# Retention values: the mean over a head's channels taken off the weights by GpSimd, in the recurrent passes, in place of a centring matmul on TensorE

## The reference, cut to what matters

```python
def group_norm_heads(z, eps):
    mu = jnp.mean(z, axis=-1, keepdims=True)
    var = jnp.mean(jnp.square(z - mu), axis=-1, keepdims=True)
    return (z - mu) * lax.rsqrt(var + eps)

# retention_mixer, 8 heads: q, k with 64 channels, v with 128; chunks of 128 tokens
    def step(R, inp):
        qc, kc, vc = inp
        s = jnp.einsum('bihd,bjhd->bhij', qc, kc) * decay_mask
        inner = jnp.einsum('bhij,bjhe->bihe', s, vc)
        cross = jnp.einsum('bihd,bhde->bihe', qc * q_decay, R)
        R = R * chunk_decay + jnp.einsum('bjhd,bjhe->bhde', kc * k_decay, vc)
        return R, inner + cross
    o = group_norm_heads(o, RET_GN_EPS).reshape(B, T, RET_V_WIDTH)
    return jax.nn.silu(g) * o
```

## Time and profile before

| | us |
|---|---|
| median of three runs (2323.48 to 2326.77) | 2326.6 |
| the profiled execution's own time | 2324.7 |
| its span, first to last instruction | 2322.9 |
| TensorE busy | 2285.8 (98%) |
| TensorE weight loads | 1883.9 (81%) |
| VectorE busy | 1399.6 (60%) |
| GpSimd busy | 916.8 (39%) |
| ScalarE busy | 752.9 (32%) |

### The profile page before, as it was taken

The page is one execution under the profiler, slowest core; times in us unless marked ns, Lnnn a source line. Parts: engine busy times, 40 slices in busy tenths (PEclk is TensorE's granted clock), DMA queues, the critical chain, the costliest instruction groups (busy, mean ns, idle before and its releaser), DMA issues.

```text
span 2322.9 us, 33491 instructions
## 1 busy us (share of the span) xinstructions
PE 2285.8 (98%) x12764; PEld 1883.9 (81%) x12764; DVE 1399.6 (60%) x1632; ACT 752.9 (32%) x1243; POOL 916.8 (39%) x538
## 2 busy tenths in 40 slices
PE   7999999999999999999999999999999999999998
PEld 6788888888888888888888877888888887777776
DVE  7755374537543754576638895555551488756775
ACT  4311131122111211334325224444432445114442
POOL 3311231123112313403366457777744445422164
PEclk9999999999999999999999999999999999999999
DMA  3211211121111113663544422222156433211023
GB/s 148 80 55 46 74 55 55 55 74 55 55 55 65 64 46 117 204 225 136 190 148 136 175 94 82 82 82 82 64 196 213 144 123 100 67 57 43 31 82 118
DMA packets 71317, 230.65 MB, mean 99 GB/s; under 512 B 6800, under 2 KB 11024, under 8 KB 70672
## 3 DMA queue, kind: packets, MB, share of 16 engines
q1 hardware_dynamic: 40560, 138.76, 18.2%
q10 hardware_dynamic: 30624, 89.97, 10.5%
HBM read 182.04 MB, written 46.66 MB: 98 GB/s over the span
## 4 chain that ended last, share of the span: by engine, by line
PE 86%; DVE 7%; ACT 2%; issue 1%; DVEq 1%; POOL 1%; DMA 1%; POOLq 1%; ACTq 0%; SPq 0%
PE psg L771 7%; PE psg L776 7%; PE psg L778 6%; PE psg L639 4%; PE psg L644 4%; PE psg L643 4%; PE psa L1243 2%; PE psa L1245 2%; PE psa L1246 2%; PE psb L1243 2%; PE psb L1245 2%; PE psb L1246 2%; PE psa L871 2%; PE psb L858 1%; PE psg L733 1%; PE psg L1454 1%
## 5 line engine op out<-in xcount | busy, mean ns | idle before, releaser
L527 POOL CAST whi<-wraw 128x1024 fp32r<-128x1024 f32 (+1 forms) x144 | 166.7, 1158 | 1102.5 <-PE psg L771 512.2
L529 POOL TENSOR_TENSOR wlo<-wraw,whi 128x1024 fp32r<-128x1024 f32 (+1 forms) x144 | 370.6, 2574 | 20.8 <-issue 0.2
L771 PE MATMUL psg<-xhi,whi 128*128 128x512 f32 x640 | 259.2, 405 | 0.0
L778 PE MATMUL psg<-xhi,wlo 128*128 128x512 f32 x640 | 258.0, 403 | 0.0
L776 PE MATMUL psg<-xlo,whi 128*128 128x512 f32 x640 | 256.4, 401 | 0.0
L639 PE MATMUL psg<-xhi,whi 128*128 128x512 f32 x496 | 196.8, 397 | 4.0 <-DVE fg L2015 2.4
L644 PE MATMUL psg<-xhi,wlo 128*128 128x512 f32 x496 | 195.2, 394 | 0.0
L643 PE MATMUL psg<-xlo,whi 128*128 128x512 f32 x496 | 194.3, 392 | 0.0
L603 POOL TENSOR_TENSOR wlo<-wraw,whi 128x1024 fp32r<-128x1024 f32 (+1 forms) x50 | 111.9, 2239 | 140.0 <-ACT whi L2799 74.2
L771 PEld LDWEIGHTS psg<-xhi,whi 128*128 128x128 f32 x640 | 120.9, 189 | 26.1 <-issue 6.3
L778 PEld LDWEIGHTS psg<-xhi,wlo 128*128 128x128 f32 x640 | 120.8, 189 | 21.0 <-issue 1.0
(11 more groups left out here) (710 smaller groups left out, 5893.5 us busy)
## 6 DMA issues: line engine op xcount, KB each, us to landing
wraw<-w SPq DMA_DIRECT2D x208, 512.0 KB, 3.5
later_scratch<-stage ACTq DMA_DIRECT2D x40, 512.0 KB, 2.6
sraw<-w SPq DMA_DIRECT2D x16, 512.0 KB, 4.0
ff_scratch<-ring ACTq DMA_DIRECT2D x10, 512.0 KB, 2.6
ff_scratch<-ff ACTq DMA_DIRECT2D x10, 512.0 KB, 2.6
ff<-ff_scratch ACTq DMA_DIRECT2D x5, 1024.0 KB, 7.0
RV<-later_scratch SPq DMA_DIRECT2D x4, 1024.0 KB, 11.5
RG<-later_scratch SPq DMA_DIRECT2D x4, 1024.0 KB, 5.5
```

The costliest lines, as they stand in the source:

```text
L527: pool.tensor_copy(whi[:, u, 0:width], wraw[:, u, 0:width])
L529: pool.tensor_tensor(wlo[:, u, 0:width], wraw[:, u, 0:width], whi[:, u, 0:width].bitcast(F32), ALU.subtract).then_inc(w_ready, 1)
L771: mm = pe.matmul(ps[:, cols], whi[:, slot, w_cols], xhi[:, k, cols], start=(k == 0), stop=False)
L778: mm = pe.matmul(ps[:, cols], wlo[:, slot, w_cols], xhi[:, k, cols], start=False, stop=(k == KT - 1))
```

## The change

The two value blocks of each recurrent pass are split by a new function, `centre_block`. It adds up the 128 columns of each of the block's eight tiles by halving (three additions over 8 x 32 elements per partition, then five over 8 x 16, 8, 4, 2 and 1), scales the eight sums by 1/128, subtracts them from the weights (1024 elements), and then casts and subtracts as `split_block` does, with a drain between any two. The retention values then come out with no mean, and `ret_values` turns them with a plain transpose. The matrix `RC`, its DMA and its row in the constants are gone; the small buffer of the sums lies where it lay. GpSimd's loop over the passes has all 14 blocks of a pass in its body, where it had two.

```diff
+            def centre_block(i, u):
+                raw = wraw[:, u, :].rearrange("p (k c) -> p k c", c=P)
+                pool.wait_ge(w_landed[u], 16 * i + 16)
+                pool.wait_ge(w_used, 2 * i + u + 1)
+                pool.sem_inc(go, 1)
+                part = w_part
+                n = P // 4
+                pool.tensor_tensor(part[:, :, :], raw[:, :, 0:n], raw[:, :, n:2 * n], ALU.add)
+                for c in (2, 3):
+                    pool.drain()
+                    pool.tensor_tensor(part[:, :, :], part[:, :, :], raw[:, :, c * n:c * n + n], ALU.add)
+                n //= 2
+                while n:
+                    pool.drain()
+                    pool.tensor_tensor(part[:, :, 0:n], part[:, :, 0:n], part[:, :, n:2 * n], ALU.add)
+                    n //= 2
+                pool.drain()
+                pool.tensor_scalar(part[:, :, 0:1], part[:, :, 0:1], 1.0 / P, None, ALU.mult)
+                pool.drain()
+                pool.tensor_tensor(raw, raw, part[:, :, 0:1].broadcast_to([P, KT, P]), ALU.subtract)
+                pool.drain()
+                pool.tensor_copy(whi[:, u, :], wraw[:, u, :])
+                pool.drain()
+                pool.tensor_tensor(wlo[:, u, :], wraw[:, u, :], whi[:, u, :].bitcast(F32), ALU.subtract
+                                   ).then_inc(w_ready, 1)
...
-            split_blocks(2, B_BRW)
+            with pool.Fori(0, PAIRS) as p:
+                for q in range(RW_B // 2):
+                    for u in range(2):
+                        if q == VALUE_PAIR:
+                            centre_block(RW_B // 2 * p + q + 1, u)
+                        else:
+                            split_block(RW_B // 2 * p + q + 1, u)
...
-            sp.dma_start(RC[:, :], mats[:, M_CENT_RET, :]).then_inc(sem("rv_in"), 16)
...
-                    pe.wait_ge(sem("rv_in"), 16 * p + 32)
+                    pe.wait_ge(sem("rv_in"), 16 * p + 16)
...
-                    mm = pe.matmul(dst[:, c, :], RV[:, h, c * P:c * P + P], RC[:, :], start=True, stop=True)
+                    mm = pe.transpose(dst[:, c, :], RV[:, h, c * P:c * P + P], m(M_ID))
```

More of the change, by code:

```diff
@@ L56 @@
 NMAT = M_LVL + LEVELS
-M_CENT_RET = NMAT
 LATER = 10
@@ L63 @@
 RW_B, RW_T = 4 + LATER, 6 + LATER
+VALUE_PAIR = 3
 B_BRW, T_BRW = B_RW + RW_B * PAIRS, T_RW + RW_T * PAIRS
@@ L282, in build @@
         RKT, RS = tiles("RKT", 24, [P, NB, P]), tiles("RS", 25, [P, NB, P])
-        RP, RC = [tiles("RP0", 26, [P, NB, P]), spare("RP1", 6, [P, NB, P])], at("RC", arena + 27 * 4096 + 3072, [P, P])
+        RP = [tiles("RP0", 26, [P, NB, P]), spare("RP1", 6, [P, NB, P])]
+        w_part = at("w_part", arena + 27 * 4096 + 3072, [P, KT, P // 4])
         rraw = [tiles("rraw_first", 4, [P, 2, T]), tiles("rraw1", 18, [P, 2, T]), spare("rraw0", 0, [P, 2, T])]
@@ L3186, in constants @@
     t, s = i[:, None], i[None, :]
-    mats = np.zeros((NMAT + 1, P, P), np.float32)
+    mats = np.zeros((NMAT, P, P), np.float32)
     mats[M_ID] = np.eye(P)
@@ L3190, in constants @@
     mats[M_CENT] = np.eye(P) - same / CH
-    mats[M_CENT_RET] = np.eye(P) - 1 / P
     mats[M_BLK] = same
```

## The result

The change makes the kernel slower by 0.36%: the ratio of the times is 1.0036, with a 95% interval of 1.0027 to 1.0045. The median of 8 runs is 2333.34 us (2331.62 to 2336.9) against 2325.48 us (2323.48 to 2327.99, 8 runs too) of the kernel before. The interval makes the loss 6.3 to 10.5 us, 8.4 in the middle. The forecast was 2339.1 us, 12.5 more than the 2326.6 of the three runs that it started from; the sign and the range held, the size was too large. The profiled execution took 2333.42 us with a span of 2331.6, which is 8.7 over the span before.

The account below looks back on a forecast made before the run. TensorE, with 86% of the chain, was taken to bound the kernel. Waits of 9.6 us plus 4.2 of clock less 1.3 of retention made 12.5 us over the 2326.6 median: 2339.1 us, range 2327 to 2356.

Parts of the forecast that it names:

- The mechanism and the place: In each recurrent pass, GpSimd and VectorE exclude each other on SBUF; TensorE waits for `centre_block` at the third later feature.
- Block 7: Second value block of each pass: ends by 348 us, hidden with 4 us to spare before its feature at about 352.
- The scores: TensorE's scores in each pass, which wait for VectorE's preparation (L1729): claimed not to be late.
- The wait's size: TensorE's wait for the first value block: 2.4 us per pass, 9.6 us in four; bounds 1.6 and 3.3 per pass.
- The block's own length: A centred value block alone on GpSimd: 11.4 us, against 3.6 before.
- The turns: Block 6 beside VectorE's preparation: 0.45 us late start, then six long VectorE instructions slip in, 0.8 us added each, 4.8 in all.
- The clock: TensorE drops to the 1.2 GHz level behind new waits, 1.7 us each, counted in 2.5 passes: 4.2 us (bounds 0 and 6.8).
- Retention: Three junctions of retention passes, values turned by transposes: 0.43 us gained each, 1.3 us in all; bounds 0.8 and 5.9.
- The two heads of the first pass: Retention stage: their shorter turning saves nothing, since TensorE then waits 2.85 us for GpSimd until 962.35 and would wait longer.
- (a): Rival: GpSimd's short instructions needn't wait for VectorE's long ones, so no pass waits; 2325.3 us, or up to 2320.7; chance 0.13.
- (b): Rival: GpSimd's short instructions over eight rows cost 0.3 us more each, 2352.5 us, or 0.6 more, 2363.3; chance 0.15.
- (c): Rival within the forecast's range: waits never cost the clock, or are short; 2331.7 to 2334.9 us; chance 0.72 together with the forecast.

Follow-up runs that it names:

- `centre_only`: The changed kernel with the value blocks centred but the values still turned by the matmul with `RC`; ratio to the kernel before 1.0038 (1.0024 to 1.0052), 8.8 us.

## Why the prediction was right, and where it was off

**The mechanism and the place: right.** One wait per pass for the last subtraction of `centre_block`, at the first matmul of the third later feature. TensorE was ready 338.10 - 2.02 - 321.75 = 14.33 us after GpSimd's start (14.26 forecast). Block 7 was hidden: it ended at 350.09, 6.2 us before GpSimd could begin block 8 (4 forecast). The scores weren't late.

**The wait's size: 2.0 instead of 2.4.** The block's own length came out right, 11.32 against 11.4, but by two errors: the short instructions together took 0.3 us more than forecast (the scaling of 8 elements 0.24 for 0.23, the additions of 128 to 8 elements 1.93 for 1.58), and the subtraction of the means took 1.92 us where the row of another two-input subtraction over 1024 elements gave 2.39. The turns cost 4.90 instead of 5.25: six slips of 0.8 were forecast, in the rows it is 1.62 for two and 2.86 for the other four. Between two of VectorE's long instructions there stands a short copy (L1748), which I had left out; that GpSimd gains the missing 0.35 there is argued, not shown. And 0.13 us pass from GpSimd's end to TensorE's start. 16.22 + 0.13 - 14.33 = 2.02; four make 8.1, not 9.6.

**The clock: +1.7 net instead of 4.2.** This is the step that was mis-sized. 2.5 passes of four were counted; two had it in this profile, one in its second execution, one in `centre_only`: 4 of 12 waits of 2.0 us. And the count left out that the half level behind L1012, which stood in the kernel before, could go. With the rows as they were nothing told that it would. What a stretch costs, 1.7 us, was right. (Of the 5.8 us between forecast and median another 1.1 is the start: 2326.6 was the median of three runs, 2325.48 that of eight.) Here the rows spoke against the Trainium skill, and the runs still do: "TensorE: Matmul & The Clock Gate", section "HAM oscillation — how this bites in real kernels", lets only idle gaps longer than these cost the clock, and half-level stretches stood behind waits of 2.0 us. My 4.2 was no better a guide: 8 of the 12 waits of 2.0 us cost nothing.

**Retention: -1.35 us, forecast -1.3.** Junction by junction, -0.45 for -0.43. The two heads of the first pass gave nothing, but for another reason than the one given: TensorE waits for the values' copy by ScalarE (L1058 for `RVT`) 2.2 us where it waited 1.3, so the 0.9 us were turned into a wait before L1012 was reached.

**The rivals.** (a), that short instructions slip past VectorE's long ones for nothing, fell: beside VectorE's long ones they waited their turns. (b), that short instructions over eight rows are dear, fell too: 0.74 us for 256 elements as forecast; the row of the undisturbed block has nothing added. The Trainium skill, "GPSIMD Engine Reference", section "Performance pitfalls for Q7 kernels", prices small read commands; the estimate from its figure was some 0.7 us more for each instruction, which the 0.74 us row doesn't show. (c), waits without the clock's loss, 2331.7 to 2334.9 us, is the one that the time came to, 2333.3, and that is partly luck: the clock did cost 3.4 us behind two waits of the profiled run, and a stretch that went elsewhere, shorter waits and a lower start made up for it. I held (c) apart from the forecast only by name, and should have given the likeliest time nearer to it.

**Two slips in the sums.** Six times 0.97 us is 5.8, not 5.9, and with a fixed part of 0.30 us the wait comes to 3.0 to 3.2 us, not 3.3. The forecast hangs on neither.

## What to carry to other kernels

Work given to GpSimd is costed by its neighbours, not by its length: ask whether VectorE reads two SBUF tensors at that time, and add, for each of its long instructions, its hold less the gap that passes anyway (0.7 to 0.8 us here), however short the GpSimd instruction is that waits. The same ten added instructions a block cost 8 us in one slot of the pass and nothing that could be measured two slots later, so when a step is moved to an idle engine, its place is a choice as large as the move. And where work is taken off the busiest engine between two answers of another, read who is late next: here 5.9 us of matmuls were worth 1.35, and moving one product of VectorE behind the answer was worth 1.7.

## What the runs showed of the hardware that was not expected

- A GpSimd subtraction over 1024 elements whose second operand is one value per row of 128, read again and again, takes 1.92 us, against 2.39 with two full operands. Five additions over 128, 64, 32, 16 and 8 elements take 1.93 us together, the shortest 0.205; one over 256 takes 0.74.
- The half level of TensorE's clock isn't tied to a wait of a given length. Behind waits of 2.0 us it stood 4 times in 12, behind those of 3.2 us 3 times in 4 and longer, behind one and the same wait of 2.8 us in one of the six profiles that have it, and in another pass when the same kernel ran again.
- A slower TensorE can go with a shorter stage: where the half level delayed TensorE's products by 1.4 us, VectorE's long instructions came behind GpSimd's, and 2.8 us of waiting were gone. And a half level behind one wait (2.4 us, L672) left the next at 1.6 us where it was 3.2 without, in six profiles against four, with both seen of the same kernel.
